# Neighbourhood attention in column strips, with q, k, v and bias laid out ahead, and the last projection in the same block

## The reference

```python
row_start = jnp.clip(jnp.arange(rows) - kh // 2, 0, rows - kh)                  # kh = 8
col_idx = jnp.clip(jnp.arange(GRID_W) - kw // 2, 0, GRID_W - kw)[:, None] + jnp.arange(kw)   # kw = 16
...
s_loc = jnp.einsum('bqhd,biqjhd->bhqij', q_r, k_win) * scale + bias
s_ctx = jnp.einsum('bqhd,bchd->bhqc', q_r, k_c) * scale
p = jax.nn.softmax(jnp.concatenate([s_loc.reshape(...), s_ctx], axis=-1), axis=-1)
o = jnp.einsum('bhqij,biqjhd->bqhd', p_loc, v_win) + jnp.einsum('bhqc,bchd->bqhd', p_ctx, v_c)
...
y = (o * jax.nn.silu(g)) @ w_out
x = x + gate * y
return rms_norm(x, final_g)
```

## Time and profile before

| what | value |
|---|---|
| median of 3 runs | 1812.83 us (1812.78 to 1813.06) |
| profiled execution | 1809.4 us, its span 1807.4 us |
| mean granted TensorE clock | 0.976 |
| PE / PEld busy | 1671.0 us (92%) / 1407.3 us |
| DVE / ACT / POOL busy | 903.5 / 854.2 / 338.9 us |
| moved by DMA | 164.26 MB in 132602 packets, 91 GB/s |

### The profile page before, as it was taken

One profiled execution on the slowest core, in us unless ns is written; L12 is line 12 of the kernel. 1 busy time (PEld: TensorE's weight loads), 2 busy tenths in 40 slices (PEclk: granted clock), 3 DMA queues, 4 the chain that ended last, 5 costly groups with the idle time before them and its releaser, 6 DMA issues. The chain is left out here.

```text
span 1807.4 us, 28173 instructions
## 1 busy us (share of the span) xinstructions
PE 1671.0 (92%) x10128; PEld 1407.3 (78%) x10128; DVE 903.5 (50%) x2273; ACT 854.2 (47%) x2024; POOL 338.9 (19%) x252
## 2 busy tenths in 40 slices
PE   7699999998999999899999999999598898888698
PEld 3176778897999988788788888899477777777586
DVE  1612212216888888644210001111488888888654
ACT  4211221216777777555321112100288888888621
POOL 0211110002222111000200000000245555555100
PEclk9899999999999999999999999999699999999899
DMA  7455411409600000322132223300233333332343
GB/s 282 137 177 174 128 51 46 141 31 163 87 16 16 16 15 16 120 82 71 59 116 96 91 83 108 112 13 1 69 88 100 95 83 93 99 99 64 130 155 112
DMA packets 132602, 164.26 MB, mean 91 GB/s; under 512 B 49474, under 2 KB 104852, under 8 KB 132500
## 3 DMA queue, kind: packets, MB, share of 16 engines
q1 hardware_dynamic: 132500, 162.86, 31.0%
HBM read 115.65 MB, written 39.26 MB: 86 GB/s over the span
## 5 line engine op out<-in xcount | busy, mean ns | idle before, releaser
L1811 PE MATMUL p<-h_hi,w_hi 128*128 128x512 f32 (+1 forms) x448 | 168.5, 376 | 2.6 <-POOL w_lo L2003 2.6
L1812 PE MATMUL p<-h_lo,w_hi 128*128 128x512 f32 (+1 forms) x448 | 168.3, 376 | 0.0
L1813 PE MATMUL p<-h_hi,w_lo 128*128 128x512 f32 (+1 forms) x448 | 168.1, 375 | 0.0
L598 PE MATMUL pp<-h_hi,w_hi 128*128 128x512 f32 (+1 forms) x432 | 156.8, 363 | 8.6 <-PEq L122 8.6
L1308 PE MATMUL nTB<-ident,nprob 128*128 128x128 f32 x768 | 132.5, 282 | 32.7 <-DVE pt_mid_lo L1492 10.5
L600 PE MATMUL pp<-h_hi,w_lo 128*128 128x512 f32 (+1 forms) x432 | 153.7, 356 | 0.0
L599 PE MATMUL pp<-h_lo,w_hi 128*128 128x512 f32 (+1 forms) x432 | 153.7, 356 | 0.0
L1060 ACT ACTIVATE prob<-S,nm,qk_inv 128x512 f32<-128x512 f32 (+1 forms) x208 | 146.4, 707 | 8.3 <-DVE nm L996 8.3
L1308 PEld LDWEIGHTS nTB<-ident,nprob 128*128 128x128 f32 x768 | 87.8, 141 | 76.8 <-DVE pt_mid_lo L1492 29.0
L1968 DVE TENSOR_TENSOR w_lo<-w_raw,w_hi 128x1024 fp32r<-128x1024 f32 x22 | 27.0, 1226 | 227.2 <-ACT w_hi L1892 227.2
L1298 PE MATMUL nS<-k_split,q_split 128*128 128x256 f32 (+2 forms) x320 | 109.0, 368 | 31.8 <-DMA k_swapped<-k_split 20.0
(11 more groups left out here) (256 smaller groups left out, 4778.9 us busy)
## 6 DMA issues: line engine op xcount, KB each, us to landing
w_raw<-in_na_w_in SPq DMA_DIRECT2D x13, 1024.0 KB, 6.5
wmod<-in_mod_w SPq DMA_DIRECT2D x24, 512.0 KB, 4.6
wside<-in_mod_w SPq DMA_DIRECT2D x12, 1024.0 KB, 5.1
k_swapped<-k_split SPq DMA_DIRECT2D x32, 320.0 KB, 4.0
w_raw<-in_ga_w_in SPq DMA_DIRECT2D x9, 1024.0 KB, 5.6
bias_scratch<-in_bias SPq DMA_DIRECT2D x16, 476.2 KB, 16.1
bias_end<-bias_scratch SPq DMA_DIRECT2D x32, 224.0 KB, 4.5
gate_scratch<-g_stage SPq DMA_DIRECT2D x8, 640.0 KB, 3.1
```

The source lines that it names most:

```text
L598: pe.matmul(acc, whi[:, k, ws], hi[:, k, a:a + width], start=(k == 0), stop=False)
L1811: pe.matmul(ps[:, bank, 0:width], whi[:, k, ws], hi[:, k, a:a + width], start=(k == 0), stop=False)
L1812: pe.matmul(ps[:, bank, 0:width], whi[:, k, ws], lo[:, k, a:a + width], start=False, stop=False)
L1813: last = pe.matmul(ps[:, bank, 0:width], wlo[:, k, ws], hi[:, k, a:a + width], start=False, stop=(k == KT - 1))
```

## The change

In grouped attention the skewed bias goes. SP instead fills a table `bias_table` in DRAM, for every head, three kinds of strip and two halves of the grid a full 128 x 384 block: `bias_fill` copies the mask value to the gaps and to `bias_wide`, `bias_space` puts the 16 taps of each column in their places, and `bias_rows` moves 8 grid rows of taps to each of the query rows. The loads of the gate input are now written out one by one with these moves between them.

In `out_and_second_projections` q and k are split at eviction: ScalarE writes the high part, VectorE the low part, in the order of four column strips of 16 queries, or of 32 key columns, in three slots; each goes to DRAM with its own store (a k tile has 3 items of 2 stores). The gate is stored in strip order. A V tile is now copied by ScalarE and subtracted by VectorE to `vstage` (three slots) and stored in DRAM, no longer kept in SBUF. Before the V stores SP loads the 4 MB of last output weights, and GpSimd multiplies them by the layer's gate row and splits them while V is computed.

`neighbourhood_and_out` takes the place of the last two blocks. A unit is one of 4 strips by one of 8 head pairs; it has 4 steps (2 heads by 2 halves of the grid), each 128 queries (8 rows by 16 columns) by 12 x 32 local keys and 256 ctx keys, all in one PSUM row of 640, 128 steps in all. One instruction on VectorE adds the bias and takes the minimum of the negated scores; exp has scale -1. From step 36 on each step also has three matmuls of 512 columns of the last projection, so that a tile of 128 tokens takes 16 steps. The last 39 steps of the loop have no scores. Everything is unrolled. x and the output have one slot, q, k, v and the gate two, the bias three sets of one head each.

The core of the diff:

```diff
--- before.py
+++ after.py
-                for head in range(NH):
-                    src = bass.AP(tensor=io["bias"].tensor, offset=head * BIAS_ROWS * BIAS_W, ...)
-                    sp.dma_start(dst, src).then_inc(skewed, 16)
-                with sp.Fori(1, QH) as h:
+                bias_fill(sp, io, filled, tabled)
+                for h in range(1, QH):
                     load(h)
+                    if h == 1:
+                        sp.wait_ge(filled, 16)
+                    if h <= KINDS:
+                        bias_space(sp, io, h - 1, spaced)
+                    if h == KINDS + 1:
+                        sp.wait_ge(spaced, 16 * KINDS * STRIP_W)
+                    if KINDS < h <= KINDS + HALVES:
+                        bias_rows(sp, io, h - KINDS - 1, tabled)
...
+                def last_weights():
+                    sp.wait_ge(mm2, NT)
+                    for i in range(3):
+                        sp.wait_ge(stored[i], stored_by(ITEMS + (i - ITEMS) % 3))
+                    for k in range(KT):
+                        sp.dma_start(w1_raw[:, k, :], w_out1[k * P:(k + 1) * P, :]).then_inc(w1l[k], 16)
...
+        LAG = 2
+        PV = LAG + 3
+        OUT = PV + 1
+        O1 = 4
...
+                def bias_in(gr):
+                    s, i, a, _, _ = place(2 * gr)
+                    if gr >= SETS:
+                        sp.wait_ge(mxd, 2 * (gr - SETS) + 2)
+                    to = bias[:, gr % SETS, :]
+                    for f in range(HALVES):
+                        at = f * (LOCAL + NCTX)
+                        sp.dma_start(to[:, at:at + LOCAL], io["bias_table"][2 * i + a, KIND[s], f]).then_inc(bl[gr % SETS], 16)
+
+                def inputs(u):
+                    s, i, slot = u // PAIRS, u % PAIRS, u % 2
+                    heads = slice(2 * i, 2 * i + 2)
+                    tok = slice(s * 256, s * 256 + 256)
+                    if u >= 2:
+                        sp.wait_ge(qkd, 4 * (u - 2) + 4)
+                    sp.dma_start(ka[:, slot, :, :].bitcast(F32), io["kl"][heads, :, s, :]...).then_inc(qkl[slot], 16)
+                    sp.dma_start(qs[:, slot, :, :].bitcast(F32), io["qd"][heads, :, tok]...).then_inc(qkl[slot], 16)
+                    for b in range(2):
+                        sp.dma_start(qx[64 * b:64 * b + 64, slot, :, :].bitcast(F32), ...).then_inc(qkl[slot], 16)
+                    if u >= 2:
+                        sp.wait_ge(pvd, 2 * (u - 2) + 2)
+                        sp.wait_ge(gid, 2 * (u - 2) + 2)
+                    grid = io["vd"][NCTX:, i, :].rearrange("(r w) d -> r w d", w=GRID_W)
+                    for b in range(4):
+                        sp.dma_start(vs[:, slot, b, :].bitcast(F32), grid[4 * b:4 * b + 4, FIRST_COL[s]:FIRST_COL[s] + KEY_W, :]).then_inc(vl[slot], 16)
+                    sp.dma_start(vs[:, slot, 4:6, :].bitcast(F32), io["vd"][0:NCTX, i, :]...).then_inc(vl[slot], 16)
+                    sp.dma_start(g[:, slot, :], io["gl"][i, :, tok]).then_inc(vl[slot], 16)
...
+                for u in range(UNITS):
+                    if u == 0:
+                        sp.dma_start(kc[:, :, :].bitcast(F32), io["kc"].rearrange("h p n -> p h n")).then_inc(kcl, 16)
+                    bias_in(2 * u)
+                    inputs(u)
+                    bias_in(2 * u + 1)
+                    if u == 1:
+                        sp.dma_start(gain[:, :], ...).then_inc(gl, 16)
+                        x_in(0)
+                    n = u - PAIRS - 7
+                    if n >= 0 and n % 4 == 0:
+                        x_out(n // 4)
+                        x_in(n // 4 + 1)
...
+                for p in range(END):                       # TensorE
+                    q = p - LAG
+                    if p < STEPS:
+                        scores(p)
+                    if 0 <= q < STEPS:
+                        turn(q, 0)
+                        turn(q, 1)
+                    gr = (p - PV + 1) // 2
+                    if 0 <= gr < STEPS // 2:
+                        product(gr, (p - PV + 1) % 2 == 1)
+                    if o_step(p):
+                        out_project(*o_step(p))
...
+                def fold(gr):                              # ScalarE, last in steps 2 * gr + 6
+                    _, _, a, _, _ = place(2 * gr)
+                    act.wait_ge(pvd, gr + 1)
+                    if gr >= 2:
+                        act.wait_ge(sumd, gr - 1)
+                        act.wait_ge(gid, gr - 1)
+                    act.copy(inv[rows(a), :], O[rows(a), gr % 2, 256:512]).then_inc(invd, 1)
+                    act.copy(half[rows(a), :], O[rows(1 - a), gr % 2, 0:256]).then_inc(halfd, 1)
...
+                def residual(tile, b):
+                    dve.wait_ge(om, 16 * tile + 8 * b + 8)
+                    cols = slice(512 * b, 512 * b + 512)
+                    dve.wait_ge(xl, 16 * (tile + 1))
+                    dve.tensor_tensor(x[:, cols], acc[:, b, :], x[:, cols], ALU.add).then_inc(x2d, 1)
...
+                for p in range(END):                       # VectorE
+                    q = p - LAG
+                    if p < STEPS:
+                        biggest(p)
+                    if p >= OUT and (p - OUT) % 2 == 0 and (p - OUT) // 2 < STEPS // 2:
+                        unite((p - OUT) // 2)
+                    done = o_step(p - 1)
+                    if done and done[2] == PAIRS - 1:
+                        residual(done[0], done[1])
+                    if 0 <= p - 1 < STEPS:
+                        reciprocal(p - 1)
+                    if 0 <= q < STEPS:
+                        low(q, 0)
+                        low(q, 1)
...
+            @block.gpsimd
+            def _(pool):
+                for gr in range(STEPS // 2):
+                    pool.wait_ge(invd, gr + 1)
+                    ...
+                    pool.tensor_tensor(gi[rows(a), :], inv[rows(a), :], g[rows(a), slot, :], ALU.mult).then_inc(gid, 1)
```

More of the change, by code:

```diff
@@ L1805, in tile @@
                     else:
[L1806 removed]
+                        evicted(pe, n - 2)
                     if n == KT:
@@ L1820, in _ @@
                     tile(n)
+                pe.wait_ge(scd, N)
+                for k in range(KT):
+                    last = pe.transpose(ps[:, 4 + k // 4, (k % 4) * P:(k % 4 + 1) * P],
+                                        mod[:, 1, 16 + k, 0:1].broadcast_to([P, P]), consts["ident"][:, :])
+                last.then_inc(g1t, 1)
                 for i in range(VB):
@@ L2065, in _ @@
+                for tile in range((UNITS - 1 - PAIRS - 7) // 4 + 1, TILES):
+                    x_out(tile)
+                    if tile + 1 < TILES:
+                        x_in(tile + 1)
+                sp.wait_ge(st, 16 * TILES)
             @block.tensor
             def _(pe):
-                for k in range(KT):
-                    last = pe.transpose(ps[:, 4 + k // 4, (k % 4) * P:(k % 4 + 1) * P],
-                                        mod[:, 1, 16 + k, 0:1].broadcast_to([P, P]), consts["ident"][:, :])
@@ new lines, in out_project @@
+                def out_project(tile, b, k):
+                    s, f = tile // 2, tile % 2
+                    if f == 0 and b == 0:
+                        pe.wait_ge(old, PAIRS * s + k + 1)
+                    if k == 0 and tile:
+                        pe.wait_ge(x2d, 2 * (tile - 1) + b + 1)
+                    tok, cols = slice(f * P, (f + 1) * P), slice(512 * b, 512 * b + 512)
+                    pe.matmul(acc[:, b, :], ohi[:, s % 2, k, tok], w_hi[:, k, cols], start=(k == 0), stop=False)
+                    pe.matmul(acc[:, b, :], ohi[:, s % 2, k, tok], w_lo[:, k, cols], start=False, stop=False)
+                    last = pe.matmul(acc[:, b, :], olo[:, s % 2, k, tok], w_hi[:, k, cols], start=False, stop=(k == PAIRS - 1))
+                    last.then_inc(om, 1)
@@ new lines, in norm @@
+                def norm(tile):
+                    act.wait_ge(x2d, 2 * tile + 2)
+                    if tile:
+                        act.wait_ge(st, 16 * tile)
+                    act.activation(work[:, :], x[:, :], ACT.Square, accum_out=ss[:, tile:tile + 1]).then_inc(sqd, 1)
+                    act.wait_ge(sqd, tile + 1)
+                    act.activation(root[:, tile:tile + 1], ss[:, tile:tile + 1], ACT.Sqrt, bias=consts["eps"][:, :],
+                                   scale=1.0 / D).then_inc(rtd, 1)
@@ new lines, in unite @@
+                def unite(gr):
+                    _, _, a, _, _ = place(2 * gr)
+                    dve.wait_ge(halfd, gr + 1)
+                    if gr >= 2:
+                        dve.wait_ge(od, gr - 1)
+                    dve.tensor_tensor(summed[rows(a), :], O[rows(a), gr % 2, 0:256], half[rows(a), :], ALU.add).then_inc(sumd, 1)
+                def residual(tile, b):
[3 more added lines that the diff above has]
+                    dve.tensor_tensor(x[:, cols], acc[:, b, :], x[:, cols], ALU.add).then_inc(x2d, 1)
```

985 lines of the change are left out of this document (409 added, 576 removed).

## The result

2468.65 us after the change (2461.86 to 2472.54, 4 runs), 1812.94 before in the same comparison: a ratio of 1.361 [1.359, 1.363], 36% slower. The forecast was 1863 in a range of 1793 to 1903. The sign is right, the size is off by 606 us. The profiled execution has a span of 2466.7 us where the forecast's sum has 1857.9.

A forecast was written before the change was run, and what follows sets the result against it. Old attention: a ring of handovers, no engine full; new: a serial DMA chain of 15.0 us a unit. With residual inputs, norms and tail, 576.7 us replace 526.2, +50.5 on 1812.8: 1863 us, range 1793 to 1903.

The forecast's parts named there:

- ordinary units: Attention units without residual input: 11.6 us until the transfers land plus 3.4 to gate_inv, 15.0 us each.
- all that hides, and 6 stores a k tile with it: Second projection: longer evictions and the stores lie under the matmuls, 11 us even for the shorter q tile.
- The burst: Attention: 14 transfers a unit on SP's queue, 2.75 MB, take 9.7 us, landing after 11.6 with the fixed part.
- 14.0: it does not decide: Attention: the second chain, through the bias loads, takes 1.9 + 4.6 + 7.5 us a unit, under 15.0.
- The wait that replaces it: Attention: SP waits for gate_inv once a unit with later bias, k and q behind it, a serial chain of 15.0 us.
- DMA share of 0.6 or more: Sign expected in the attention if the forecast holds; the kernel before had 0.31 there.
- The residual input: Attention: five late loads block VectorE, making a unit 22.8 us plus 0.2, 8 us extra each, 40 us in all.
- The norms: ScalarE in five attention steps: 4.1 us of work, 3 hidden in the unit's wait, 1 us each, 5 in all.
- (A): Rival, attention: transfers run at full rate, bias loads decide, 12.7 us a unit, 1794 us in all; chance 0.19.
- (B): Rival, attention: TensorE falls to 1.2 GHz between transfers, adding 1.2 us a unit, 36 us, 1899 in all; chance 0.2.
- (C): Rival, attention: transfers hide as if V and bias were asked for early, 1720 us in all; chance 0.04.
- the ring: Attention: handovers between engines set 2.75 us a step, 3.05 with the out projection, 11.0 and 12.2 a unit.

The follow-up runs named there:

- stores16: Changed kernel with each store of split q and k cut into one per head, 64 rows each: 2051.61 us, ratio 1.132.
- vload16: Changed kernel with the four V strip loads of a unit cut to start with 32 columns instead of 4 grid rows: 2384.92 us, ratio 1.316.
- order: Changed kernel with SP issuing the next bias, k and q before the gate_inv wait, V and gate after it: 2292.62 us, ratio 1.265.
- all4: Changed kernel with stores per head, V loads by 32 columns, SP's new order, and residual store and load one unit earlier: 1803.52 us, ratio 0.994.
- final_a: all5_late_x16 with residual input behind next unit's bias, k and q but before the gate_inv wait, output store behind V and gate: 1735.71 us, ratio 0.958.
- all5_late: all5 with VectorE's sum of the two halves one step later, behind the next minimum: 1789.58 us, ratio 0.986.
- all5_late_x16: all5_late with residual input and output store each cut into 8 transfers of 16 rows, input ahead of the store: 1754.92 us, ratio 0.967.
- all5: all4 with output store and residual input moved between the two bias inputs, ahead of the gate_inv wait: 1815.03 us, ratio 1.000.

## Why the prediction was wrong, step by step

The error is 2466.7 - 1857.9 = 608.8 us of span, and it adds up:

| step of the sum | forecast | measured | error |
|---|---|---|---|
| second projection, end to end | +0.9 | 1165.8 to 1596.9, +431.1 | +430.2 |
| V | 115.4 | 116.9 | +1.5 |
| V's end to SP's first wait over | 19.4 + 27.4 | 52.9 | +6.1 |
| 25 ordinary units | 25 x 15.0 | 487.9 | +113 |
| 4 units with residual input | 4 x 23 | 133.0 | +41 |
| norms, in the units | 4 | in the two rows above | -4 |
| from the last wait on | 15 + 1 + 8 + 34 | 79.2 | +21 |

- **The step that failed** is "all that hides, and 6 stores a k tile with it". I compared the evictions with the matmuls, found them shorter (they are), and let the stores go by without a term. The 27.3 MB of q and k stores on 2 engines take 606 us at the 45 GB/s of the k tiles, twice the 287 us of matmuls that should have covered them. The test that the prediction named, second projection more than 3 us longer, came out at 429. stores16 takes 417 of them back.
- **The burst** of 2.75 MB had the right size and order; its rate was read from the earlier trace rows, where 16 engines work. With V on 16 engines that rate holds: 2.75 MB in 12.0 us less the fixed 1.9 is 272 GB/s. The landing of the V strips on 4 engines was the mis-sized term: 19.5 us a unit, 16.6 with V on 16, the forecast 15.0. The last 1.6 are of the size of what the chain under vload16 shows (0.4 until q has landed, 1.1 behind it). "14.0: it does not decide" was wrong for the bias chain for the same reason: with V on 4 engines the bias decides.
- **The wait that replaces it**, one gate_inv a unit and k, q and bias behind it, was right in its place (30 waits at that line) and is shown by order. The units before and with the out projection are alike (18.4 to 20.0 and 18.5 to 21.3), as forecast. Of the signs that the prediction named, the DMA share of 0.6 or more in the attention failed: it is 0.44.
- **The residual input** was right as a wait of VectorE (114.0 us, 7 times) and mis-sized: 13.7 us a unit more than an ordinary one in place of 8. vload16, with V out of the way, has it at 15.1. The transfers run on 8 engines, and in the tail, where I had no term, two of them stand bare at 10.1 us each.
- **The norms** were sized right as work (4.1 us). In after no unit with a norm stands out, so they lie in the wait of the unit, as I said; it is the faster kernels that pay, 4.7 to 5.9 us for one in all4.
- **Rivals.** (A) needed the full rate, and no run of after's layout had it. The fit that I cited for it from the Trainium skill (DMA: Bandwidth & Descriptors, Anatomy of one DMA) is given there for DMAs that GpSimd issues; here SP issues them, and the transfers that mattered ran on few engines. (B) did come in part: the granted clock in after's attention is 0.78, between its two levels of 1.2 and 2.4 GHz, and in vload16's chain the work after the landing takes 1.1 us more than forecast. It rides on the waits and goes when they go (1.00 in all4 from 1367 to 1469). (C) had 1720 us if the burst hides. final_a, which comes nearest to hiding it, takes 1736, but with a shorter ring (all5_late) and with norms and residual inputs that still cost; that the two numbers are so close is partly luck.
- The size of a transfer, which the forecast weighed, did not decide: the stores of 512 KB were the slow ones, and pieces of 256 KB the fast ones. The shape decided.

Still open: how final_a's 378 us divide between transfers (share 0.88) and the ring. No experiment changed the bytes.

## What to carry to other kernels

Look at the outermost dimension of each DMA before its bytes: with 2 there, these stores had 2 of the 16 engines. Cutting such a transfer into pieces that start with 16 or more (64 in stores16, 16 in all5_late_x16) paid here in spite of the added issues. A wait for DMAs at a low DMA share is the sign, 0.14 with 2 engines here. In a queue with one order, put a transfer with a wait of its own behind all those that could go now; and where a moved transfer has to pass others, count what it does to them (all5 gained nothing).

## What the hardware showed that I had not expected

- A backlog on 2 engines stops the issuing queue: SP's issue of such a store took 10.8 us in the median, against 0.64 in stores16. A load behind them, itself spread wide, is caught too. The weight loads of after among its DMA issues (count, KB, median us from issue to landing; 6.5 before):

```profile
w_raw<-in_na_w_in SPq DMA_DIRECT2D x11, 1024.0 KB, 18.8
```

The same of stores16:

```profile
w_raw<-in_na_w_in SPq DMA_DIRECT2D x11, 1024.0 KB, 8.0
```

- One engine moves 22 GB/s in stores of 1 KB rows (45 GB/s on two), between its shares of the 264 and 397 GB/s in the earlier trace rows, 16.5 and 24.8: these stores weren't slow per engine, they only had few. For the 8-engine pair in the tail this isn't shown: 1 MB in 10.1 us is 13 GB/s an engine, 16 if the fixed 1.9 us of the prediction is taken off, which is at or below the lower of the two.
- TensorE that waits for such stores runs its own work at a lower clock: a mean of 0.64 in the k tiles, between 1.2 and 2.4 GHz, and 0.99 when the stores are wide.
